# The start of a hybrid decoder layer: identity made on the chip, counts set by three engines, weight loads held until x is there, and parameter steps placed later

## What is computed

```python
h = rmsnorm(x, ln_gain)
z = h @ w_in            # q 16x64 | k 4x64 | v 4x64 | gate 1024 | recurrent in 1024 | recurrent gate 1024
q, k = partial_rope(q), partial_rope(k)
y_a = rmsnorm(sliding_window_attention(q, k, v, sinks) * silu(g_attn), attn_out_gain)
u = causal_depthwise_conv(x_lru, conv_w, conv_b)
r, i = sigmoid(u @ w_rgate + b_rgate), sigmoid(u @ w_igate + b_igate)     # per block of 64
a = exp(-8 * r * softplus(-lam));  hs = scan(a, sqrt(1 - a*a) * i * u)
y_l = rmsnorm(hs * silu(g_lru), lru_out_gain)
out = rmsnorm(x + concat([y_a, y_l]) @ w_out, final_gain)
```

## Time and profile before

| | us |
|---|---|
| median of 3 runs | 1385.79 (1383.7 to 1386.67) |
| the profiled execution's own time | 1386.63 |
| span of the profiled execution | 1385.0 |
| TensorE busy | 1358.6 |
| VectorE busy | 956.5 |
| ScalarE busy | 818.3 |
| GpSimd busy | 192.6 |

### The profile page before, as it was taken

How to read it: one execution, slowest core, us unless ns; L and a number is a source line. 1 busy time by engine, 2 the same in 40 slices (tenths; PEclk the granted TensorE clock), 3 DMA queues, 4 the chain that set the end, 5 groups by cost and what they waited for, 6 DMA issues and landing times.

```text
span 1385.0 us, 22262 instructions
## 1 busy us (share of the span) xinstructions
PE 1358.6 (98%) x6756; PEld 1108.2 (80%) x6756; DVE 956.5 (69%) x1663; ACT 818.3 (59%) x1695; POOL 192.6 (14%) x250
## 2 busy tenths in 40 slices
PE   8999999999999999999999999999999999999998
PEld 7777877788888888888888888888877888888886
DVE  6798989877686777778687767777786534444442
ACT  6878696857667585757667485766764321213120
POOL 2020202111120212112030211112120000000000
PEclk9999999999999999999999999999999999999999
DMA  9575857754545556464546565454635423233220
GB/s 340 189 259 200 303 198 278 254 191 168 186 170 182 195 174 219 151 203 149 205 164 213 174 232 196 152 187 171 213 113 176 152 76 106 90 92 112 69 91 31
DMA packets 98433, 243.29 MB, mean 176 GB/s; under 512 B 8128, under 2 KB 43200, under 8 KB 98368
## 3 DMA queue, kind: packets, MB, share of 16 engines
q1 hardware_dynamic: 91344, 217.86, 46.0%
q0 software_dynamic: 7024, 24.65, 4.7%
HBM read 179.56 MB, written 62.91 MB: 175 GB/s over the span
## 4 chain that ended last, share of the span: by engine, by line
PE 76%; DVE 8%; ACT 8%; issue 5%; DMA 1%; ACTq 0%; DVEq 0%; POOL 0%; SPq 0%; POOLq 0%
PE ring L1482 42%; PE acc_b L204 12%; PE ring L204 11%; PE ps_v L1536 3%; PE ps_s L1515 3%; PE ring L1549 2%; ACT p_sb L843 1%; PE ps_t L1523 1%; ACT w_hi L703 1%; DMA w_raw<-w_tiles_d 1%; DVE w_lo L1031 1%; DVE hs L1324 1%; DVE o_sb L1256 1%; PE ring L1559 1%; DVE ya L1264 1%
## 5 line engine op out<-in xcount | busy, mean ns | idle before, releaser
L1482 PE MATMUL ring<-split,w_hi 128*128 128x512 f32 x2288 | 717.5, 395 | 3.9 <-DVE w_lo L1031 2.8
L1482 PEld LDWEIGHTS ring<-split,w_hi 128*128 128x128 f32 x2288 | 421.2, 188 | 100.2 <-issue 7.3
L1482 PE MATMUL ring<-split,w_lo 128*128 128x512 f32 x1144 | 446.8, 391 | 0.0
L1482 PEld LDWEIGHTS ring<-split,w_lo 128*128 128x128 f32 x1144 | 214.7, 188 | 46.0
L629 POOL TENSOR_SCALAR_AFFINE_SELECT p_hi_c<-p_hi 128x512 fp32r<-128x512 f32 x64 | 40.6, 635 | 707.5 <-ACT p_hi L851 707.5
L1281 DVE SCALAR_TENSOR_TENSOR cu<-xl,prm,cu 128x512 f32<-128x512 f32 x96 | 72.0, 750 | 47.7 <-ACT cu L870 42.8
L843 ACT ACTIVATE p_sb<-s_sb,smax 128x129 f32<-128x129 f32 x256 | 99.5, 390 | 0.6
L1760 ACT ACTIVATE w_hi<-res 128x1024 fp32r<-128x1024 f32 x15 | 15.9, 1059 | 134.1 <-DVE res L1830 134.1
L204 PE MATMUL acc_b<-wo_rest,y_own 128*128 128x512 f32 x384 | 91.3, 394 | 2.5 <-DVE wo_rest L165 2.2
L204 PE MATMUL ring<-split,y_own 128*128 128x512 f32 x384 | 91.4, 393 | 0.5 <-DVE split L165 0.5
L204 PEld LDWEIGHTS acc_b<-wo_rest,y_own 128*128 128x128 f32 x384 | 72.7, 190 | 18.8 <-DVE wo_rest L165 3.0
(11 more groups left out here) (239 smaller groups left out, 2382.4 us busy)
## 6 DMA issues: line engine op xcount, KB each, us to landing
w_hi<-w_split_scratch SPq DMA_DIRECT2D x108, 512.0 KB, 3.3
w_lo<-w_split_scratch SPq DMA_DIRECT2D x108, 512.0 KB, 4.3
w_raw<-w_tiles_d SPq DMA_DIRECT2D x36, 512.0 KB, 4.7
w_split_scratch<-w_hi SPq DMA_DIRECT2D x36, 512.0 KB, 5.3
w_split_scratch<-w_lo SPq DMA_DIRECT2D x36, 512.0 KB, 6.0
y_scratch<-hs POOLq DMA_DIRECT2D x32, 256.0 KB, 4.2
y_scratch<-ya POOLq DMA_DIRECT2D x16, 512.0 KB, 7.8
rows<-y_scratch SPq DMA_DIRECT2D x8, 1024.0 KB, 7.6
```

The source lines that it names most:

```text
L1482: last = mm(bank(r), w[:, i % WSLOTS, k, :], h[:, par, k, :], start=(k == 0 and j == 0), stop=(k == KC - 1 and j == 2))
```

## The change

Five edits, all ahead of the first group:

1. The identity is no longer loaded. GpSimd makes it out of a zeroed tile: where the column equals the partition, it fills in 1.
2. Priming is shared by GpSimd, VectorE and TensorE, a third each. TensorE's warm-up is 8 products instead of 12.
3. SP issues the parameters ahead of KVG, and waits for block 2 of x before Q0's load and for block 3 before Q1's.
4. VectorE does the first two parameter steps between blocks 1 and 2 of x.
5. ScalarE's exponential and logarithm with their table loads come after the split of XL1, and it copies q out of PSUM ahead of `keep_k`. VectorE's step between them comes after XL1's split, and its 13 last steps come after the first q's low part.

```diff
-            sp.dma_start(ident[:, :], identity).then_inc(ident_in, 16)
...
+            sp.dma_start(prm[:, 0:C_GAIN + 1, :], channel_params).then_inc(prm_in, 16)
             load_group(-1, KVG, 0)
-            sp.dma_start(prm[:, 0:C_GAIN + 1, :], channel_params).then_inc(prm_in, 16)
+
+            sp.wait_ge(pro_x_in[2], 16)
             load_group(-1, Q0, 0)
+            sp.wait_ge(pro_x_in[3], 16)
             load_group(-1, Q1, 0)
...
             nc.gpsimd.memset(v_carry[:, :, :], 0.0).then_inc(zeroed, 1)
-            for s in primed[0::2]:
+            pool.wait_ge(zeroed, 2)
+
+            nc.gpsimd.affine_select(out=ident[:, :], in_=v_carry[:, 0:P // HD, :].rearrange("p g c -> p (g c)"),
+                                    compare_op=ALU.not_equal, fill=1.0, base=0, pattern=[[1, P]],
+                                    channel_multiplier=-1).then_inc(ident_made, 1)
+            for s in primed[0::3]:
...
             take_kv(-1)
+            split_w(-1, NG + XL0)
+            high_k(-1)
+            take_q(-1, 0)
+            keep_k(-1, 0)
+            split_w(-1, NG + XL1)
             act.wait_ge(prm_step, 2)
             nc.scalar.activation(prm[:, C_T1, :], prm[:, C_T0, :], ACT.Exp).then_inc(prm_act, 1)
-            split_w(-1, NG + XL0)
             act.wait_ge(prm_step, 3)
             nc.scalar.activation(prm[:, C_T2, :], prm[:, C_T0, :], ACT.Ln).then_inc(prm_act, 1)
 
             nc.scalar.activation(xs[:, 2:3], ones[:, :], ACT.Exp).then_inc(x_early_root, 1)
-            high_k(-1)
-            keep_k(-1, 0)
-            take_q(-1, 0)
-            split_w(-1, NG + XL1)
             high_q(-1, 0)
...
-            for s in primed[1::2]:
+            for s in primed[1::3]:
                 dve.sem_inc(s.sem, s.prime)
...
             for b in range(NBLK):
+                if b == 2:
+                    dve.wait_ge(prm_in, 16)
+                    done(nc.vector.tensor_scalar(col(C_T1), col(C_LAM), -1.0, None, ALU.mult))
+                    done(nc.vector.tensor_tensor(col(C_T0), col(C_LAM), col(C_T1), ALU.min))
                 dve.wait_ge(pro_sq, b + 1)
...
-            done(nc.vector.tensor_scalar(col(C_T1), col(C_LAM), -1.0, None, ALU.mult))
-            done(nc.vector.tensor_tensor(col(C_T0), col(C_LAM), col(C_T1), ALU.min))
             dve.wait_ge(table_in, 32)
             dve.wait_ge(zeroed, 5)
             turn_k(-1, 0)
-            dve.wait_ge(prm_act, 1)
-            done(nc.vector.tensor_scalar(col(C_T0), col(C_T1), 1.0, None, ALU.add))
             dve.wait_ge(*w_low.at(-1, NG))
             split_w(-1, NG + XL0)
...
+            turn_q(-1, 0)
+            split_w(-1, NG + XL1)
+            dve.wait_ge(prm_act, 1)
+            done(nc.vector.tensor_scalar(col(C_T0), col(C_T1), 1.0, None, ALU.add))
+            add_q(-1, 0)
+            low_q(-1, 0)
             dve.wait_ge(prm_act, 2)
...
-            turn_q(-1, 0)
-            split_w(-1, NG + XL1)
-            add_q(-1, 0)
-            low_q(-1, 0)
             turn_q(-1, 1)
...
+            for s in primed[2::3]:
+                pe.sem_inc(s.sem, s.prime)
             pe.wait_ge(zeroed, 2)
-            warm(12)
-            pe.wait_ge(ident_in, 16)
+            warm(8)
+            pe.wait_ge(ident_made, 1)
```

More of the change, by code:

```diff
@@ L216, in hymba_kernel @@
 def hymba_kernel(nc, x, ln_gain, w_tiles, sinks, w_gates, w_out, final_gain, channel_params, out_gains,
-                 rope_cos, rope_sin, first_cap, identity, out):
+                 rope_cos, rope_sin, first_cap, out):
     y_dram = nc.dram_tensor("y_scratch", (EC, P, SEQ), F32, kind="Internal").ap()
@@ L250, in hymba_kernel @@
         done_a = phase_a(nc, top, block, both, signals_b, proj, x, ln_gain, w_tiles, sinks, w_gates,
-                         channel_params, out_gains, rope_cos, rope_sin, first_cap, identity, y_dram, ws_dram)
+                         channel_params, out_gains, rope_cos, rope_sin, first_cap, y_dram, ws_dram)
         phase_b(nc, block, both, signals_b, proj, done_a, x, final_gain, out)
 def phase_a(nc, top, block, both, signals_b, proj, x, ln_gain, w_tiles, sinks, w_gates,
-            channel_params, out_gains, rope_cos, rope_sin, first_cap, identity, y_dram, ws_dram):
+            channel_params, out_gains, rope_cos, rope_sin, first_cap, y_dram, ws_dram):
     ident, ones, egain = both.ident, both.ones, both.egain
@@ L342, in phase_a @@
         pro_x_in = [sem(f"pro_x_in{b}") for b in range(NBLK)]
-        ident_in = sem("ident_in")
+        ident_made = sem("ident_made")
         prm_in = sem("prm_in")
@@ L1053, in low_x, with done @@
                                         ALU.subtract).then_inc(*done)
+            col = lambda c: prm[:, c, :]
+            step = [0]
+            def done(ins):
+                step[0] += 1
+                ins.then_inc(prm_step, 1)
+                dve.wait_ge(prm_step, step[0])
             for b in range(NBLK):
+                if b == 2:
+                    dve.wait_ge(prm_in, 16)
+                    done(nc.vector.tensor_scalar(col(C_T1), col(C_LAM), -1.0, None, ALU.mult))
+                    done(nc.vector.tensor_tensor(col(C_T0), col(C_LAM), col(C_T1), ALU.min))
                 dve.wait_ge(pro_sq, b + 1)
@@ L1069, in _ @@
             split_w(-1, KVG)
-            dve.wait_ge(prm_in, 16)
             for c in range(KC):
@@ L1148, in low_v @@
                                         ALU.subtract).then_inc(*dv_low.one())
-            col = lambda c: prm[:, c, :]
-            step = [0]
-            def done(ins):
-                step[0] += 1
-                ins.then_inc(prm_step, 1)
-                dve.wait_ge(prm_step, step[0])
-            done(nc.vector.tensor_scalar(col(C_T1), col(C_LAM), -1.0, None, ALU.mult))
-            done(nc.vector.tensor_tensor(col(C_T0), col(C_LAM), col(C_T1), ALU.min))
             dve.wait_ge(table_in, 32)
@@ L1999, in constants @@
     cap[:, 0, :][prev] = NEG
-    return {"rope_cos": cos, "rope_sin": sin, "first_cap": cap,
-            "identity": np.eye(P, dtype=np.float32)}
+    return {"rope_cos": cos, "rope_sin": sin, "first_cap": cap}
 def laid_out(inputs):
```

## The result

| | before | after |
|---|---|---|
| median, us | 1385.52 (15 runs, 1383.7 to 1387.39) | 1387.21 (15 runs, 1386.46 to 1391.41) |
| ratio to before | | 1.0017, 95% interval 1.0009 to 1.0025 |
| the profiled execution's own time | 1386.63 | 1387.21 |
| its span | 1385.0 | 1385.5 |
| first product with h | 15.94 | 16.93 |

What follows compares the result with a forecast made beforehand. TensorE, busy 98%, could gain only at the start, through the gates' release by the VectorE and ScalarE chain. First product -1.5 plus chain +0.6 gave -0.9 us: 1384.9 on the median's scale, range 1382.6 to 1387.4.

Steps and rivals of the forecast that it cites:

- What bounds the kernel: Start, to 45 us: an earlier first product counts only as it moves the gates' release, set by VectorE and ScalarE.
- The select: GpSimd's 128x128 identity select replacing the 64 KB load: 0.3 us taken, bounds 0 and 0.64.
- L = 1.7: What the landings of x and later loads move without the identity's load: 1.7 us earlier, bounds 0 and 2.4.
- The rival that the landings do not move: First loads: the landing gap belongs to the queue, not the identity; +1.1 us, 1386.9; chance 0.22.
- the one in which the chain gains too: Start through second q: first product 1.8 earlier, chain 0.6 shorter; -2.4 us, 1383.4; chance 0.22.
- Priming, cost 0: TensorE's 35 increments ahead of warm-up: 2.6 us, start about 3.5, over by 6.7, hidden, cost 0.
- The third rival: TensorE's clock still low at the first product, through the key/value product: about +4 us, 1389.9; chance 0.05.
- S = 1.5: What the first product with h moves: 1.5 us earlier; 1.8 or -0.5 at the landings' two ends.
- The hold, cost 0: SP's waits before Q0's and Q1's loads: nothing gained for x, no cost behind them; other end 1.9 us.
- c = 0.6: What the chain from first product to second q loses to moved table loads and 13 steps: 0.6 us, ends -0.6 and +1.6.
- The sum: At the gates: -1.5 + 0.6 = -0.9 us, 1384.9 on the median's scale; stall grows from 1.92 to 2.5.
- The falsifier: Block 2 landing at 9 or later, or gates after 47, would prove the landings or chain term wrong.

Runs made afterwards that it cites:

- steps back: Changed kernel without SP's two waits for x, priming by GpSimd and VectorE, warm-up 12, edit 5 undone; ratio to before 1.0001 (0.9992 to 1.001).
- steps on GpSimd: Changed kernel, two engines priming, no SP waits; 12 of VectorE's 13 last steps and one before on GpSimd, exponential ahead of k's high part; 1385.14 us, ratio 0.9998.
- two engines priming: Changed kernel with edit 2 undone (GpSimd and VectorE prime half each, warm-up 12): 1385.63 us, ratio 1.0004; also 1.0004 without SP's two waits.
- the one with the same instructions named above: Changed kernel plus seven idle identity products of TensorE ahead of the first gates, first group's TensorE instructions written ahead of the loop; 1386.15 us, ratio 1.001.
- the one with both undone: Changed kernel with edits 2 and 5 undone, SP's two waits for x kept; 1386.48 us, ratio 1.001 (1.0001 to 1.0018).
- the control: Kernel before with edit 1 alone and the first group's TensorE instructions written ahead of the loop, no idle products; 1384.86 us, ratio 0.9999.

## Why the prediction was wrong, point by point

**What bounds the kernel** was read rightly: the gates' release, moved by what stands before it, went the way of the time (+2.24 there, +1.7 in the median). But "Behind it all three engines keep their order and shift together" was not so: with the clock lost behind the stall the shift was 3.07 at the next transposes.

**The select** (0.3 taken) took 0.29.

**L = 1.7** was 1.3 at block 2 (8.0 against 9.30; 1.6, at 7.66, in two kernels without the hold), inside its bounds: the gap in the landings was largely the identity's. The rival that the landings do not move falls, and so does the one in which the chain gains too.

**Priming, cost 0, is the step that failed.** "TensorE gets 35 ahead of its warm-up, 2.6 us, and starts at about 3.5" took GpSimd's 0.073 for an increment over to another engine. GpSimd again took 0.07 (36 in the 2.54 before its memset at 4.34), but TensorE started at 6.33: with the old start of 1.33 that is 5.0 for 35, 0.14 each, and up to 5.4 if TensorE began its increments at 0.93, when ScalarE began. From that came "over by 6.7" (it was 9.8), transposes that began 1.7 after the identity's old landing, at the low clock, and a first product at 16.93 instead of 14.4. (The 16 passes were priced at 0.198 each; that was a mean over both levels of the clock, at the low one they take 0.218.) The cover was named ("Block 0 is normed before 7.9 as now"), but the duration had no upper bound, although no row of the trace showed an increment of TensorE. Two kernels show the price both ways: 2.05 and 0.98 at the first product, 1.67 and 1.23 at the gates; of the two further pairs one agrees (2.41, 2.63), the other at the first product alone (1.41, -0.53).

**The third rival** was near the mechanism and had the wrong point of decision. The clock did rise late, by the weight loads shortly before 12.20, but before the 14.4 where I had it begin to matter. It matters from the first transpose: block 0's and the products of zeros between the blocks took 9.66 to 12.20, 2.5 us, where block 1's took 12.20 to 13.51. The Trainium skill, "TensorE: Matmul & The Clock Gate", Part 1, has the engine throttled by default and released by activity. The trace agrees: with the warm-up later and thinner it stayed at the lower level for longer.

**S = 1.5** holds without edit 2 and the hold: 15.94 - 14.43 = 1.51. The two other kernels with the same instructions up to there give 1.85 (steps back) and 1.11 (steps on GpSimd), so 1.5 was hit within a scatter of 0.4 either way. The identity alone gives 1.84, so the earlier parameters and edit 4 add nothing that shows. VectorE's step ahead of block 2's mean did have an idle time ahead of it, 1.03 at 9.48, and block 3's square came at 10.18, not 9.7.

**The hold, cost 0, is a second step that was wrong, though its price in the changed kernel does not show.** "All were landed long before use" counted the tables, constants and gains, and was right for them. It left out that the DMA engines go short (266 GB/s from 10 to 13 us against 401), and that a store issued later goes behind the delayed loads. The wait was priced as a delay of what stands behind it on SP and not as bytes lost. At the gates the pairs give 1.3 and 3.0 where the product is early, and in the changed kernel 0.4, which is within scatter. That it gives x nothing was right: block 2 is squared at 7.66 without it, 8.04 with it. The Trainium skill, "DMA: Bandwidth & Descriptors", section "Queues, rings and completion order", has descriptors taken in ring order; by that rule later loads take nothing from x, and these two rows agree.

**c = 0.6** was 0.54 without the hold and with two engines priming, 0.2 to 0.9 between the changed kernel's instructions and those with the steps put back, and -0.7 in the pair with hold and two engines priming: right in the middle, with a scatter as large as itself. The whole chain lost 1.25 in the profiled execution (0.58 in the one with the same instructions named above). The part beyond c is the wait of XL0's rounding, which I moved in front of the table loads at no cost, and which met the store that the first of them had covered. I had read "its first table load begins" at 22.48 as a cost to be gained and not as the cover of a wait that no row shows.

**The sum** -1.5 + 0.6 became, at the gates, +0.99 + 1.25 = +2.24.

**The falsifier** worked half: it said that gates after 47 would prove L or c wrong. They came at 49.02, and L and c were not what was wrong. It had no place for an error in a term that had been set to 0.

**Still open.** The kernel with the identity alone reaches the gates 1.56 earlier than the kernel before and is not measurably faster. Its clock falls after the stall; that of the kernel before did not fall there in the profiled execution, but fell near 1047 us. Of the 14 profiled executions three lost it there, behind stalls of 1.9 to 2.2 us, and eleven did not, behind stalls of 1.2 to 2.4. So one profile does not say where a kernel usually loses its clock, and the mean clock of the other executions of the kernel before (mostly 0.997 and 0.998) fits a loss at either place. That the early start is given back by the clock is therefore argued from profiles and not shown in the times. A kernel in which TensorE does its increments behind the warm-up was not tried.

## What to carry to other kernels

An increment, a wait or a copy has a price per engine: a duration from one engine's row is no price for another, and a term moved to an engine that stands ahead of a critical chain needs an upper bound even when it looks hidden. A wait on a loading queue costs the bytes that are not moved meanwhile, and the next store that something waits for can pay for them. Before an operation is moved out of a place, ask which silent wait it was covering there; and a start made earlier is worth little if the next stall lets the clock fall, so look at the granted clock behind each stall that stays. And before a difference of half a microsecond between two profiles is given a cause, compare two kernels with the same instructions up to that point: here they differed by 0.5 at the gates.

## What the runs showed of the hardware

- TensorE took 5.0 to 5.4 us for 35 increments of semaphores (0.14 to 0.15 each), GpSimd 2.54 for 36 (0.07 each), in the same execution.
- A stall of 1.6 to 2.1 us of TensorE at the first gates was followed by some 3.4 us at the 1.2 GHz level in the profiles of the changed kernel and of most variants (in the one with both undone 6.8, beginning at about 45.9, with stalls of 1.88 and 2.02 on either side of twelve short products), and not in those of the kernel before (stall 1.92) and of the one with the steps on GpSimd (1.61), while the control lost it with 1.65. Near 1045 us, at a stall of the output projection, three of the 14 profiled executions lost the clock (stalls of 1.92, 1.99 and 2.23) and eleven kept it (1.19 to 2.42). The length of the stall alone does not decide it. With 1.83 us of idle products in the stall at the gates it did not happen there in either kernel.
- GpSimd's steps on 128x8 numbers took 0.20 to 0.72 us each, VectorE's 0.16 to 0.20.
